# Two plain pairs instead of three in feed-forward blocks 2 and 3, earlier accumulating transfers, a silu moved, and Ln with Exp for the reciprocal root

## The reference, cut to what matters

```python
x = x + 0.5 * swiglu(rms_norm(x, g), w_gate, w_up, w_down)   # blocks 0 to 3, D_FF = 2816
swiglu(x) = (silu(x @ w_gate) * (x @ w_up)) @ w_down
rms_norm(x) = x * rsqrt(mean(x * x) + 1e-6) * gain
```

## Time and profile before

| | before |
|---|---|
| median of 3 runs | 1954.88 us |
| profiled execution | 1955.77 us |
| span of the profiled execution | 1954.0 us |
| TensorE busy | 1948.1 us (100%) |
| VectorE busy | 1397.9 us (72%) |
| ScalarE busy | 851.6 us (44%) |
| GpSimd busy | 527.3 us (27%) |

### The profile page before, as it was taken

One profiled execution on the slowest core, in us unless ns is written; L12 is line 12 of the kernel. 1 busy time (PEld: TensorE's weight loads), 2 busy tenths in 40 slices (PEclk: granted clock), 3 DMA queues, 4 the chain that ended last, 5 costly groups with the idle time before them and its releaser, 6 DMA issues.

```text
span 1954.0 us, 28996 instructions
## 1 busy us (share of the span) xinstructions
PE 1948.1 (100%) x11722; PEld 1707.3 (87%) x11722; DVE 1397.9 (72%) x1882; ACT 851.6 (44%) x1230; POOL 527.3 (27%) x394
## 2 busy tenths in 40 slices
PE   9999999999999999999999999999999999999999
PEld 7999998877789999988999998877777888999997
DVE  7877776554588877768877776773458657877773
ACT  6443333535554344345433444442546345333431
POOL 1322222142223322223322322200015413322221
PEclk9999999999999999999999999999999999999999
DMA  6556663351346666545666653232200235666653
GB/s 211 155 164 171 173 168 95 119 181 55 88 126 176 174 172 167 147 129 145 178 166 172 181 151 114 97 96 88 76 1 1 87 116 160 177 173 168 178 141 107
DMA packets 112469, 265.92 MB, mean 136 GB/s; under 512 B 10321, under 2 KB 22865, under 8 KB 112337
## 3 DMA queue, kind: packets, MB, share of 16 engines
q1 hardware_dynamic: 92336, 225.72, 35.3%
q0 software_dynamic: 19856, 38.28, 12.5%
q10 hardware_dynamic: 144, 0.09, 0.0%
HBM read 259.32 MB, written 4.72 MB: 135 GB/s over the span
## 4 chain that ended last, share of the span: by engine, by line
PE 98%; DVE 1%; DMA 0%; issue 0%; ACT 0%; SPq 0%; POOL 0%; DVEq 0%
PE BANKS L656 12%; PE BANKS L658 12%; PE BANKS L657 12%; PE BANKS L579 11%; PE BANKS L580 11%; PE BANKS L581 11%; PE BANKS L709 6%; PE BANKS L710 6%; PE BANKS L711 6%; PE BANKS L1022 2%; PE BANKS L850 1%; PE BANKS L852 1%; PE BANKS L851 1%; PE BANKS L999 1%; PE BANKS L1005 1%; PE BANKS L813 1%
## 5 line engine op out<-in xcount | busy, mean ns | idle before, releaser
L656 PE MATMUL BANKS<-BF,ASH 128*128 128x256 f32 x876 | 248.0, 283 | 0.0
L658 PE MATMUL BANKS<-BF,ASL 128*128 128x256 f32 x876 | 247.9, 283 | 0.0
L657 PE MATMUL BANKS<-BFL,ASH 128*128 128x256 f32 x876 | 247.9, 283 | 0.0
L579 PE MATMUL BANKS<-XH,HI 128*128 128x512 f32 x624 | 245.7, 394 | 0.7 <-DVE XL L1593 0.3
L1657 DVE TENSOR_TENSOR LO<-RING,HI 128x1024 fp32r<-128x1024 f32 (+2 forms) x204 | 216.3, 1060 | 41.2 <-ACT HI L1160 39.9
L580 PE MATMUL BANKS<-XL,HI 128*128 128x512 f32 x624 | 243.2, 390 | 0.0
L581 PE MATMUL BANKS<-XH,LO 128*128 128x512 f32 x624 | 243.0, 389 | 0.0
L1173 ACT ACTIVATE TMP<-TMP 128x512 f32<-128x512 f32 x88 | 55.7, 633 | 406.4 <-DVE TMP L1686 406.4
L2262 POOL TENSOR_TENSOR TMP<-TMP,RSTD 128x512 f32<-128x512 f32 x88 | 132.0, 1499 | 365.3 <-ACT TMP L1173 365.3
L2254 POOL DMA_DIRECT2D ASR<-gu_dram x73 | 88.1, 1219 | 387.5 <-DMA ASR<-gu_dram 381.5
L709 PE MATMUL BANKS<-HH,DHI 128*128 128x512 f32 x488 | 190.7, 391 | 0.0
(11 more groups left out here) (249 smaller groups left out, 4875.5 us busy)
## 6 DMA issues: line engine op xcount, KB each, us to landing
RING<-gu_dram SPq DMA_DIRECT2D x174, 512.0 KB, 3.9
ASR<-gu_dram SPq DMA_DIRECT2D x146, 256.0 KB, 2.9
ASR<-gu_dram POOLq DMA_DIRECT2D x73, 512.0 KB, 6.9
DRAW<-down_dram SPq DMA_DIRECT2D x40, 512.0 KB, 3.7
RING<-oin_dram SPq DMA_DIRECT2D x32, 512.0 KB, 3.5
RING<-down_dram SPq DMA_DIRECT2D x32, 384.0 KB, 3.2
DRAW<-down_dram SPq DMA_DIRECT2D x24, 384.0 KB, 3.7
RING<-ein_dram SPq DMA_DIRECT2D x16, 512.0 KB, 3.6
```

The costliest lines, as they stand in the source:

```text
L579: pe.matmul(PS[bank][:], HI[j][:, c], hi(k), start=(n == 0), stop=False)
L656: pe.matmul(out, w_hi[:, c], x_hi(k), start=(k == 0), stop=False)
L657: pe.matmul(out, w_hi[:, c], x_lo(k), start=False, stop=False)
L658: last = pe.matmul(out, w_lo[:, c], x_hi(k), start=False, stop=(k == 3))
```

## The change

- PLAIN is 2 for blocks 2 and 3. EARLY_FROM = (5, 4, 3, 3) keeps the early products on the pairs that had them, so pair 2 is of seven products and has no early ones.
- Units 4 and 5 are now split as parts of pair 2. On ScalarE form 3 is split ahead of the norm; then come the split of unit 4, both splits of the sums of pair 2, silu 0. VectorE has gate 0 and the sums of pair 2 behind the norm, and the splits, then up 0.
- In `block`, for blocks 2 and 3, the wait for the pair's PSUM banks stands ahead of the third product (five) and not ahead of the first.
- In pair 2 ScalarE first splits the weights and sums of pair 3, and does silu of pair 2 behind the copy of one of pair 3.
- The two first accumulating transfers of block 2 (pairs 2 and 3) are issued by GpSimd behind squares 2 and 3 in the tail of block 1; in block 3 they stay behind the squares.
- Sqrt with a reciprocal becomes Ln and then Exp with factor -0.5, all on ScalarE, in all six norms and in the four heads of the odd mixer.

```diff
-PLAIN = (5, 4, 3, 3)
+PLAIN = (5, 4, 2, 2)
+EARLY_FROM = (5, 4, 3, 3)
...
             def norm(r):
                 act.wait_ge(norm_sum, r + 1)
-                act.activation(RSTD[:], AUX[:], ACT.Sqrt, scale=1.0 / DM, bias=EPST[:]).then_inc(std_ready, 1)
+                link(act.activation(RSTD[:], AUX[:], ACT.Ln, scale=1.0 / DM, bias=EPST[:]))
+                act.activation(RSTD[:], RSTD[:], ACT.Exp, scale=-0.5).then_inc(rstd_ready, 1)
...
                     form_inputs(f, 3)
+                    form_split(f, 3)
                     norm(now)
-                    split(4, whole)
-                    form_split(f, 3)
+                    split(2 * first, whole)
+                    sums_split(first, 0)
+                    sums_split(first, 1)
                     silu(0, 1.0)
-                    split(5, whole)
-                    sums_split(first, 0)
+                    split(2 * first + 1, right)
                     h_high(0)
-                    silu(1, 1.0)
-                    split(2 * first, whole)
-                    h_high(1)
...
                     copy_one(p)
+                    ahead = f >= 2 and p == first
+                    if f >= 2 and p == first + 1:
+                        silu(p - 1, -1.0)
+                    if ahead:
+                        split(2 * nxt, whole)
+                        sums_split(nxt, 0)
+                        sums_split(nxt, 1)
...
             def norm(r):
-                dve.wait_ge(std_ready, r + 1)
-                dve.reciprocal(RSTD[:], RSTD[:]).then_inc(rstd_ready, 1)
                 dve.wait_ge(rstd_ready, r + 1)
...
                     form(f, 3)
+                    form_split(f, 3)
                     norm(now)
-                    split(4, whole)
                     gate(0)
-                    form_split(f, 3)
-                    up(0)
-                    split(5, whole)
-                    gate(1)
                     sums_second(first)
                     sums_third(first)
-                    up(1)
                 dve.wait_ge(sum_made, 2 * block_count(f, first) + 2)
                 split(2 * first, whole)
                 sums_split(first, 0)
                 sums_split(first, 1)
+                if f >= 2:
+                    up(0)
                 gate(first - 1)
                 split(2 * first + 1, right)
+                if f >= 2:
+                    sums_second(first + 1)
+                    sums_third(first + 1)
                 up(first - 1)
...
                 for m in range(KX if r is not None else 0):
                     square_tile(r, m)
+                    if f == 1 and m in (2, 3):
+                        add_pair(2, PLAIN[2] + m - 2)
```

More of the change, by code:

```diff
@@ L377, in early_index @@
         def early_index(f, p):
-            return p - PLAIN[f] - (p > ALONE[f])
+            return p - EARLY_FROM[f] - (p > ALONE[f])
         def has_early(f, p):
@@ L383, in leads @@
         def leads(f, p):
-            return has_early(f, p) and (p == PLAIN[f] or not has_early(f, p - 1))
+            return has_early(f, p) and not has_early(f, p - 1)
         def early_pairs(f):
@@ L441, in load_early @@
                     e = early_count(f, p)
-                    if p == PLAIN[f]:
+                    if p == EARLY_FROM[f]:
                         sp.wait_ge(unit_done, base + 4)
@@ L461, in block_ffn @@
                     p = n // 2 - 1
-                    if n == plain + 1:
+                    if n == plain + 1 and has_early(f, PLAIN[f]):
                         load_early(PLAIN[f])
-                    elif n % 2 and p == ALONE[f]:
+                    elif n % 2 and p >= PLAIN[f] and leads(f, p + 1):
                         load_early(p + 1)
@@ L677, in block @@
                     pe.wait_ge(lo_ready, n + 1)
-                    pe.wait_ge(bank_free, n + 2)
+                    if f < 2:
+                        pe.wait_ge(bank_free, n + 2)
                     if p == PLAIN[f]:
-                        pe.wait_ge(std_ready, r + 1)
+                        pe.wait_ge(rstd_ready, r + 1)
                         pe.wait_ge(form_lo, 4 * f + 4)
@@ L1268, in block_ffn @@
                     copy_one(p)
-                    if p == first:
+                    ahead = f >= 2 and p == first
[5 more added lines that the diff above has]
+                        sums_split(nxt, 1)
+                    if not has_early(f, p - 1):
                         h_high(p - 1)
+                    if p == first and has_early(f, p):
                         early_split(p)
-                    elif not has_early(f, p - 1):
-                        h_high(p - 1)
-                    if nxt:
+                    if ahead:
+                        split(2 * nxt + 1, right)
+                    elif nxt:
                         split(2 * nxt, whole)
@@ L1285, in block_ffn @@
                         early_split(p)
-                    silu(p, -1.0)
+                    if not ahead:
+                        silu(p, -1.0)
                     if has_early(f, p):
@@ L1451, in root @@
                         act.wait_ge(factor_ready, h + 1)
-                        act.activation(RSTD[:], RSTD[:], ACT.Sqrt).then_inc(tstd_ready, 1)
+                        link(act.activation(RSTD[:], RSTD[:], ACT.Ln))
+                        act.activation(RSTD[:], RSTD[:], ACT.Exp, scale=-0.5).then_inc(factor_root, 1)
                 def square_numerator(h, c):
@@ L1853, in block_ffn @@
                     elif nxt:
-                        sums_second(nxt)
-                        sums_third(nxt)
+                        if p == first:
+                            mid_two(p)
+                            mid_five(p)
+                            mid_three(p)
+                        else:
+                            sums_second(nxt)
+                            sums_third(nxt)
                         dve.wait_ge(sum_made, 2 * block_count(f, nxt) + 2)
                         split(2 * nxt, whole)
-                        mid_two(p)
-                        mid_five(p)
-                        mid_three(p)
+                        if p > first:
+                            mid_two(p)
+                            mid_five(p)
+                            mid_three(p)
                         sums_split(nxt, 0)
@@ L2087, in head_factor, with root_ready @@
                                              ALU.add).then_inc(factor_ready, 1)
-                def invert_factor(h):
-                    dve.wait_ge(tstd_ready, h + 1)
-                    link(dve.reciprocal(RSTD[:], RSTD[:]))
+                def root_ready(h):
+                    dve.wait_ge(factor_root, h + 1)
                 def scale_numerator(h, c):
@@ L2247, in split_unit, with add_pair @@
                 pool.tensor_tensor(LO[j][:], RAW[j][:], HI[j][:].bitcast(F32), ALU.subtract).then_inc(lo_ready, 1)
[L2249 to L2257 removed]
+            def add_pair(f, p):
+                b = p % 2
+                gate_left = gu_d[f, 2 * p, :, 0:4 * P].unsqueeze(1).to_broadcast([P, 2, 4 * P])
+                pool.wait_ge(pair_in[b], 32 * pair_count(f, p))
+                pool.dma_start(ASR[:, b, 0:2, :], gate_left, accum_op=ALU.add).then_inc(pair_sum[b], 16)
+            def block_ffn(f, r):
+                if f != 2:
+                    for p in (PLAIN[f], PLAIN[f] + 1):
+                        add_pair(f, p)
                 for p in range(FT):
                     if PLAIN[f] <= p < FT - 2:
[L2260 removed]
+                        add_pair(f, p + 2)
                     pool.wait_ge(silu_ready, 22 * f + p + 1)
```

29 lines of the change are left out of this document (12 added, 17 removed).

## The result

The changed kernel takes 1960.51 us (median of 11 runs, 1959.98 to 1961.39); the kernel before took 1955.41 in the same session (11 runs, 1954.53 to 1956.22). The ratio is 1.0026, 95% interval [1.0017, 1.0035]: slower by 0.26%, where 1956.3 and no change were forecast, and outside the range (1953.0 to 1959.2). The profiled execution took 1959.98 us, against 1955.77.

The account below looks back on a forecast made before the run. TensorE was taken as the bound, never short of work: number of matmuls times spacing. -1.64 gain + 3.1 new waits = +1.4 us, so 1957.2 profiled and 1956.3 median, no change; range 1953.0 to 1959.2.

Parts of the forecast that it names:

- The sum of the new waits: TensorE's new waits in block 2 and from the squares: 1.0 + 1.1 + 0.2 + 0.2 + 0.6 = 3.1 us, bounds 0 to 5.0.
- The gain, 0.82 us a pair: Blocks 2 and 3: one pair each from plain to seven products, 10.90 - 10.08 = 0.82 us, 1.64 in both.
- RSTD at 900.0, unit 4 at 903.3, up 0 at 907.0: Block 2's start: times in us when the norm's factor, unit 4's split and pair 0's up would be ready.
- The waits of 1.0 and 1.1: Block 2, pair 2: TensorE waits 1.0 us for unit 4's split, 1.1 before the third product for up 0.
- The one-load rival: One table load serves Ln and Exp; RSTD of block 2 ready at 898.7, 1955.1 us in all; 10% chance.
- "The split of unit 6 ... 0.2": Block 2: unit 6's split for the next pair ends, with a collision, at 914.6; TensorE wants it at 914.4, 0.2 us.
- The squares, 0.6: Block 1's tail: GpSimd's later squares meet VectorE's forms and delay its chain by 0 to 1.3 us, taken as 0.6.
- The rival for "slower": Moved accumulating transfers hold up unit 2's weights until about 885, everything behind 3 us later, 1959.4 in all; 12% chance.
- Block 3, "No wait": Block 3: unit 4 ready three us before TensorE wants it, so wait 0, bounds 0 and 1.0 us.
- The odd mixer, "I take 0": Odd mixer: roots hold ScalarE longer but TensorE has no wait there; 0 us, bounds -0.3 and +1.3.
- Blocks 0 and 1, "Nothing waits there, so 0": Blocks 0 and 1: RSTD 1.4 us earlier where the norm's sum comes last, but worth 0 us.
- the signs of being wrong: Block 2 shorter than before, or the gap at unit 2, at the norm, or in the odd mixer.

Follow-up runs that it names:

- e11: e9 with VectorE's low half of the first down tiles back behind pair 2's up, its pause there left empty; 1954.94 us, ratio 0.9999.
- e13: e11 with block 2's first two accumulating transfers issued behind the sixth and seventh of the eight squares; 1955.18 us, ratio 0.9999.
- e9: Changed kernel, block 2 reordered, Sqrt roots, transfers behind the squares, VectorE's pauses filled; ScalarE makes pair 1's high half of h later; 1955.47 us, ratio 1.0002.
- e4: Changed kernel with block 2's first two accumulating transfers issued behind all squares again; 1958.80 us, ratio 1.0018.
- e10: Changed kernel with only the odd mixer's roots by Sqrt and reciprocal again, norms kept on Ln and Exp; 1959.83 us, ratio 1.0024.
- e2: Kernel before with Ln and Exp in place of Sqrt and reciprocal, nothing else; 1955.24 us, ratio 1.0001.

## Why the prediction was wrong

The kind of thing was right: the gain per pair, where the first gaps would open, the two table loads, the squares. The sum of the new waits was too small, because it ended at pair 2 and priced the collisions there too low, and because block 3 and the odd mixer were put at nothing. Point by point:

- **The gain, 0.82 us a pair: right.** Block 3 in e11 and e13, with no stop, is 331.56 - 330.77 = 0.79 shorter.
- **RSTD at 900.0, unit 4 at 903.3, up 0 at 907.0: right to 0.5 us** (900.05, 903.35, 907.49). The waits of 1.0 and 1.1 measured 1.48 and 1.16, each with 0.1 behind it: TensorE itself came 0.4 us earlier than on the clock of before, while the chain did not. The second lies within its bound of 1.4; the first had none above 1.0.
- **The one-load rival is refuted**: all six norms have two loads of 1.28. The load at 898.13 starts 0.02 us behind the Ln's end (897.42 + 0.69): no drain shows. The Trainium skill, "ScalarE: Activation LUTs", section "Table sets: the hidden batching unit", has one load for ln then exp; this trace has two.
- **"The split of unit 6 ... 0.2": failed.** The stop stood at pair 3's second product, behind the split of its sum, and was 0.70 with 0.2 of late matmuls around it. The sum had 0.3 for a collision at up 0 and next to nothing here. Pair 3's two sums took 1.78 and 1.67 and its split 2.32 us: 3.2 over their normal 0.68, 0.69 and 1.2. For the split e9 shows that it is GpSimd; for the two sums it is argued from GpSimd's rows beside them.
- **The sum ended at pair 2: failed.** The stops of 0.19 and 0.33 at pairs 3 and 4 and the late matmuls at them, 0.8 us, have no term. VectorE's backlog is carried on, not worked off at once. The new waits are 4.64 in block 2 and 0.67 ahead of its norm, 5.3 in all: more than the upper bound of 5.0.
- **The squares, 0.6: right in size and place.** Square 4 fell onto the forms, as forecast, and square 3 onto the XL row before them. It cost VectorE 0.9 us, within the 0 to 1.3, and TensorE 0.67 of stops and late matmuls before the norm; e4 gets 0.9 back by the traces and 1.5 by the medians. The rival for "slower" had unit 2 land after 881.5, at about 885; it landed at 882.3. ScalarE waited 0.84 for it and not 3, and no stop of TensorE hung on it.
- **Block 3, "No wait": failed.** 0.62 us of stops and late matmuls, the same last ones as in block 2 (0.33 at pair 4), took most of the gain: -0.13 was left of -0.82.
- **The odd mixer, "I take 0": failed, within its bounds**: +0.9, of which 0.8 is the roots (e10). "TensorE has no wait there now" was true and said nothing about how close the chain was.
- **Blocks 0 and 1, "Nothing waits there, so 0": not quite.** Small stops too short for the list of waits stood there, and e2 shows them gone: 0.3 and 0.5 us.

Block 2 from its norm on is +3.88 where 2.5 - 0.82 = 1.68 was forecast: 2.2 more. Block 3 is 0.7 more and the odd mixer 0.9. What comes ahead of block 2's norm is -0.4 where +0.6 was forecast: 1.0 less, by blocks 0 and 1 and by a start of the program that was 0.37 shorter, which is luck. That makes 2.8 of the miss of 4.2. The other 1.4 is the step from the profiled execution to the median: 0.9 taken off, from three runs, where the median of eleven lies 0.4 below the profiled execution in the kernel before and 0.5 above it in this one, whose profiled execution was its fastest.

The range was narrower than its own parts. The upper bounds of block 2, block 3 and the odd mixer (5.0, 1.0 and 1.3) lead to 1960.5, not to 1959.2. Of the signs of being wrong one came true, a gap in the odd mixer.

## What to carry to other kernels

Price an added preparation for as many steps as the tight engine stays without a pause, not for the first step alone, and price it with the collisions that it makes itself: here three operations of a busy VectorE that ran beside GpSimd's were 3.2 us longer together. A free slot on one engine is not free when its neighbour works in it. Where two stages share one code path, look up for each what comes first, the form or the norm's sum: the order that saved 1.3 us in one block cost 1.9 in the other.

## What the runs showed of the hardware

- VectorE's operations with both inputs in SBUF are slowed when they start while GpSimd works: 512 elements 1.78 for 0.68 us, 1024 elements 2.32 for 1.22. GpSimd's own products grow from 1.28 to between 1.5 and 2.3. It depends on which began first: VectorE's split at 913.74 kept its 1.22 though GpSimd's product began 0.05 behind it; the product took 2.31, and VectorE's next split, begun during it, 2.32. An operation that reads one input from a PSUM bank isn't slowed: the residual addition of 512 elements (L1755, 128 times) takes 0.68 in the 55 cases where GpSimd works through all of it, and 0.68 without. The Trainium skill, "SBUF — State Buffer", section "Who interferes with whom", says that two SBUF inputs on VectorE contend with GpSimd's reads and that one input does not; the rows agree.
- After a stop TensorE loses 0.1 us more on the next matmul: behind the one at 903.41 the next starts at 903.63, 0.22 later and not 0.12. Three matmuls of block 2 came as late without a stop ahead of them; their cause is not shown.
- Behind accumulating transfers from GpSimd that are still under way, an ordinary load of 512 KB lands after 7.9 us in the changed kernel and 8.9 and 9.3 in e11, in place of 3.4 to 4.1. In e13 a load issued 0.5 us ahead of the first of them landed after 3.9. So which load it is, is set by where they are issued.
